# VectorE makes the low halves of all dense weights but the first six of each run of dense layers

## The reference

```python
def first_block(x, ...):
    for layer in range(2):
        h = rms_norm(x, norm_mix_g[layer])
        x = x + (mixer_ab(h, ...) if layer % 2 == 0 else mixer_rglru(h, ...))
        h = rms_norm(x, norm_ffn_g[layer])
        x = x + hierarchical_moe(h, ...)        # 32 experts, top 2 of 4 groups of 8
    return rms_norm(x, norm_final_g)

def second_block(x, ...):
    for i in range(2):
        h = rmsnorm(x, ln1_g[i]) @ w_in[i]
        (fq, fk, fv, ff, dq, dk, dv, c_q, c_kv, k_r) = jnp.split(h, split_points, axis=-1)
        o_fox  = fox_group(fq, fk, fv, ff, ...)      # 4 heads of attention with forget gates
        o_diff = diff_group(dq, dk, dv, ...)         # 4 heads of differential attention
        o_mla  = mla_group(c_q, c_kv, k_r, ...)      # 4 heads with low-rank q, k and v
        x = x + jnp.concatenate([o_fox, o_diff, o_mla], axis=-1) @ w_o[i]
        up = causal_dwconv(rmsnorm(x, ln2_g[i]) @ w_up[i], conv_w[i], conv_b[i])
        g, u = up[..., :2816], up[..., 2816:]
        x = x + (jax.nn.silu(g) * u) @ w_down[i]
    return rmsnorm(x, final_g)
```

## Time and profile before

| | |
|---|---|
| time, median of three | 2613.43 us |
| the profiled execution | 2616.33 us, span 2615.1 us |
| granted TensorE clock, mean | 0.996 |
| PE, busy | 98% |
| DVE, busy | 43% |
| ACT, busy | 35% |
| POOL, busy | 14% |
| lows (L283) on POOL | 136, 335.2 us |
| lows (L283) on DVE | 124, 200.8 us |

### The profile page before, as it was taken

How to read it: one execution, slowest core, us unless ns; L and a number is a source line. 1 busy time by engine, 2 the same in 40 slices (tenths; PEclk the granted TensorE clock), 3 DMA queues, 4 the chain that set the end, 5 groups by cost and what they waited for, 6 DMA issues and landing times.

```text
span 2615.1 us, 32699 instructions
## 1 busy us (share of the span) xinstructions
PE 2562.8 (98%) x13324; PEld 1789.3 (68%) x13324; DVE 1133.2 (43%) x1971; ACT 914.3 (35%) x1741; POOL 356.7 (14%) x160
## 2 busy tenths in 40 slices
PE   9999999999999999999989999999999999999999
PEld 7874444444777444445477778888888767888887
DVE  2543233323685233223353453552554344465264
ACT  4431111111484111111164454442345454443233
POOL 2200000000340000000030011231222002222212
PEclk9999999999999999999999999999999999999999
DMA  6248999999325999999921112232232112223222
GB/s 219 83 193 356 421 421 420 421 421 420 113 97 214 412 420 422 421 421 421 407 80 59 55 65 81 97 108 86 65 117 71 62 33 81 75 87 124 78 65 80
DMA packets 133367, 542.23 MB, mean 207 GB/s; under 512 B 13024, under 2 KB 24672, under 8 KB 84064
## 3 DMA queue, kind: packets, MB, share of 16 engines
q1 hardware_dynamic: 129264, 536.94, 52.5%
q10 hardware_dynamic: 3952, 3.17, 0.4%
HBM read 537.98 MB, written 2.10 MB: 207 GB/s over the span
## 4 chain that ended last, share of the span: by engine, by line
PE 91%; DVE 4%; DMA 2%; ACT 2%; issue 1%; POOL 0%; SPq 0%; POOLq 0%; DVEq 0%; ACTq 0%
PE ps L622 21%; PE ps L1516 16%; PE ps L624 15%; PE ps L1538 8%; PE ps L646 5%; PE ps L1492 4%; PE ps L555 4%; PE ps L2132 3%; PE ps L1553 2%; PE ps L1554 2%; DMA w<-in_moe_w_up 2%; PE ps L2089 2%; PE ps L2120 2%; PE ps L556 1%; PE ps L2111 1%
## 5 line engine op out<-in xcount | busy, mean ns | idle before, releaser
L283 POOL TENSOR_TENSOR w<-w,w 128x1024 fp32r<-128x1024 f32 (+2 forms) x136 | 335.2, 2474 | 2206.3 <-ACT w L275 2202.1
L622 PE MATMUL ps<-w,w 128*128 128x512 f32 x2592 | 590.7, 389 | 2.6 <-POOL w L283 2.6
L622 PEld LDWEIGHTS ps<-w,w 128*128 128x128 f32 x2592 | 486.1, 188 | 104.8 <-POOL w L283 3.4
L1516 PE MATMUL ps<-w,w 128*64 128x512 f32 x2048 | 445.4, 592 | 3.5 <-issue 2.0
L624 PE MATMUL ps<-w,w 128*128 128x512 f32 (+1 forms) x1872 | 408.8, 379 | 5.3 <-DVE w L541 3.0
L624 PEld LDWEIGHTS ps<-w,w 128*128 128x128 f32 x1872 | 337.9, 188 | 72.6 <-issue 5.9
L275 ACT ACTIVATE w<-w 128x1024 fp32r<-128x1024 f32 (+2 forms) x260 | 251.5, 999 | 348.9 <-PE ps L624 177.9
L283 DVE TENSOR_TENSOR w<-w,w 128x1024 fp32r<-128x1024 f32 (+2 forms) x124 | 200.8, 1626 | 350.6 <-ACT w L275 348.1
L1516 PEld LDWEIGHTS ps<-w,w 128*64 128x64 f32 x2048 | 149.0, 137 | 293.6 <-issue 293.6
L1538 PE MATMUL ps<-w,w 128*64 128x512 f32 x1024 | 226.8, 595 | 0.8 <-ACT w L1614 0.8
L1764 DVE TENSOR_TENSOR w<-ps,w 128x512 f32<-128x512 f32 x32 | 34.7, 1083 | 388.8 <-PE ps L1516 388.8
(11 more groups left out here) (257 smaller groups left out, 2471.4 us busy)
## 6 DMA issues: line engine op xcount, KB each, us to landing
w<-in_moe_w_gate SPq DMA_DIRECT2D x128, 1024.0 KB, 15.6
w<-in_moe_w_up SPq DMA_DIRECT2D x128, 1024.0 KB, 18.5
w<-in_moe_w_down SPq DMA_DIRECT2D x128, 1024.0 KB, 15.0
w<-in_w_up SPq DMA_DIRECT2D x40, 1024.0 KB, 5.1
w<-in_w_down SPq DMA_DIRECT2D x20, 1024.0 KB, 5.2
w<-in_w_in SPq DMA_DIRECT2D x16, 1024.0 KB, 5.2
w<-in_ab_w_in SPq DMA_DIRECT2D x10, 1024.0 KB, 7.6
w<-in_c_w_in SPq DMA_DIRECT2D x8, 1024.0 KB, 7.8
```

The source lines that it names most:

```text
L283: up(self.wlo[self.low[s][0]], lane.e.tensor_tensor(lo, raw, hi.bitcast(F32), ALU.subtract))
L622: ins = pe.matmul(bank[:, :], wp[:, k, P * o:P * o + P], ap(k0 + k), start=first, stop=stop)
L1516: ins = pe.matmul(bank[64 * e:64 * e + 64, :], XG[p % 3][:, 4 * u + k, 64 * e:64 * e + 64], w[e][:, k, :], start=(u == 0 and k == 0), stop ...
```

## The change

The rule for the engine is changed in one line. GpSimd keeps the first six halves of the second and third run, and of the first run the odd ones among the first six; all others go to VectorE.

```diff
                 s = len(self.halves)
                 self.halves.append((u, h))
-                engine = int(s % 2 == 1 or s < self.ring_start + NSPLIT)
+                engine = int(s < self.ring_start + NSPLIT or (s % 2 == 1 and s < NSPLIT))
                 self.n_low[engine] += 1
```

## The result

The changed kernel takes 2621.88 us, median of ten runs, against 2613.91 us for the kernel before over as many: a ratio of 1.0027, 95% interval 1.0019 to 1.0035. It is slower by 5 to 9 us. I had forecast 2615.8 us and called everything within 0.2% no change; by that bound of mine it is slower. The direction of the sum was right, its size was not. The median lies 0.9 us over the upper end of my range; by the ratio, from the 2613.43 us that I started from, it would be 2620.5 us, just inside.

A forecast was written before the change was run, and what follows sets the result against it. PE, busy for 98% of the span, was taken as the bound. Terms 0.6 + 1.5 + 2.4 + 0.8 - 2.0 - 0.9 = +2.4 us moved the median from 2613.43 to 2615.8 us; 8-in-10 range 2604.5 to 2621.

The forecast's parts named there:

- The stops: Places in mixer_ab and attention where VectorE's queue waits with a moved low for ScalarE's hi, delaying PE; +5.3 us.
- L2453: Both attention layers: a low ahead of L2453 on VectorE delays PE's L2161; +0.75 us each, 1.5 for two.
- the value product: Differential heads, both attention layers: a low delays the VectorE steps before PE's value product; +1.2 us each, 2.4 for two.
- L2407: Behind the value product, both attention layers: a low ahead of L2407 lengthens PE's wait; +0.4 us each, 0.8 for two.
- L541: mixer_ab, once: a low ahead of L541 on VectorE makes PE's L624 wait longer; +0.6 us.
- The normalization: Both attention layers: L2497, no longer held up by GpSimd's lows, finishes sooner; -1.0 us each, -2.0 for two.
- slow of itself: Rival: L2497's slowness is not GpSimd's doing, so normalization costs +4.1 instead of -1.0 per layer; 2626.0 us, chance 0.14.
- The FFN: Both layers, once: PE waits less for a low made by VectorE instead of GpSimd; -0.45 us each, -0.9 for two.
- The rest at nothing: Recurrent mixer, FFN and stage ends: new lows stand in VectorE's idle time beside long products and cost nothing.
- Stops hidden: Rival, faster: stops cost nothing, while the engines' holding each other up was on the path; 2605.0 us, chance 0.22.
- One more stop: Rival, slower: ahead of attention's gate sums, one further stop per layer is on the path; 2620.2 us, chance 0.12.
- Nothing on the path: Rival: stops and gains both lie beside PE's work; 2613.4 us, chance 0.12.

## Why the prediction was right, and where not

*The stops.* Place by place right: +5.5 us of waits against +5.3 forecast, and the kernel with the same lows one place later shows that it is the queue's order. *L2453* (1.7 against 1.5), *the value product* (2.1 against 2.4), *L2407* (1.1 against 0.8) and *L541* (0.6) each came within 0.3 us of its term.

*The normalization.* -2.1 against -2.0 between the two traces, about -1.7 when L541 is taken as the other traces have it. The 16 instructions took 4.29 us, as I had said, and the rival that took L2497 to be slow of itself has fallen. But PE got little of the gain at L541, where I had put it (-0.6 us); most came at L529, which waited for ScalarE's L2275 (-1.5 us).

*The FFN.* -1.1 against -0.9. *The rest at nothing* was right too: no new wait of PE there. VectorE's new work was mis-sized, without harm to the sum: I had 137 us; its lows took 74 us more, as a low takes 1.12 us on average after the change and took 1.62 before, and all its work 40.

*The rivals.* "Stops hidden" failed: the stops are on the path. "One more stop" did not occur: PE's waits show no such place. "Nothing on the path" failed as well: the two sides did not lie beside PE, they nearly cancelled.

*What failed: the step from waits to time.* I summed the terms to +2.4 us and took the sum for the time. The waits did add 2.3 us at these places; the time went up by 5 to 9. In my sum every microsecond of wait cost one microsecond, and TensorE's clock was not a term of it: I had put it at nothing without a reason. The runs show that behind a longer wait in the attention the granted clock often falls to 1.2 GHz for about 3 us of matmuls, about 1.5 us lost each time, and that this doubled or trebled the price of a stop: 6 us for 2.1 us of wait (one stop in each layer), 11 for 5.5 (all seven). Stretches of low clock stood in the profile of before, at 1382.3 and 2024.0 us, with a granted clock of 0.51, and I had not asked what brings them. The mean clock of 0.996 hid them.

*Luck.* That the time came out near the upper end of my range and not far beyond it is luck: that end, 2621 us, was put there for one more stop in each layer, which did not occur. The clock, which did, had no part in it.

*What stays open.* Which wait brings a stretch in a given execution: in the changed kernel the value product's start is at low clock in the first layer and not in the second, and one stretch follows in each output product, whose own wait did not change. That the longer waits at the value product and at L2161 make them more frequent is shown by the counts over the ten traces, and the mean clocks of the runs agree; by what rule they fall is not shown, nor why L2161's come in the second layer only.

## What to carry to other kernels

An instruction moved to an in-order engine costs by what stands behind it while it waits, not by its duration: of 121 moved lows, seven made the loss, and with six of these put one place later it was gone. Take the two engines' holding each other up into the sum: at the normalization it gave back about 2 us, against 5.5 us of waits at the stops. Where the profile of before already shows stretches of low clock, a wait can cost two to three times its length, as here; look for such stretches in windows of a few microseconds, not in the mean.

## What the runs showed of the hardware

- A VectorE instruction of 0.34 us with two operands in SBUF lasted 2.56 us beside a GpSimd subtraction of 2.4 us, and 0.35 us at most when no such subtraction ran beside it. VectorE's own subtractions differed as well: 124 took 200.8 us while GpSimd made 136, the longest 3.4 us; 245 took 274.5 us when GpSimd made 15, the longest 1.23 us.
- The granted clock fell to the 1.2 GHz level among the short matmuls of the attention: behind waits of 1.5 us (4 of 6 places) and 2.3 us (4 of 8) that were 0.5 and 1.5 us before, behind an unchanged wait of 1.1 us (5 of 20), and behind twenty small matmuls without a wait (9 of 20). It stayed there for about 3 us, once for nearly 7. One and the same program varied by 8 us (2615.9 to 2624.2) with its mean clock of 0.998 to 0.994.
